# Adding two of six row sets by accumulating transfers, and reordering the end of a mixture-of-experts layer

## The chip, the cores and the metric

The kernel runs on one core of a Trainium2 chip. The metric is the time of one execution on the device in microseconds. A core has TensorE (PE) for products, VectorE (DVE) and ScalarE (ACT) for elementwise work, GpSimd (POOL) and SyncE (SP). Sixteen DMA engines serve the queues: SP's and ACT's are filled by hardware, POOL's by its own software.

## What is computed

Two layers of a transformer trunk on 512 positions of width 1024, in float32. Each layer has a token mixer of four attention branches, and then a mixture of experts. What matters here is the second half:

```python
h = rmsnorm(x, norm_ffn_g[l]) * (1.0 + sc2) + sh2
h2 = h.reshape(b * s, d)
y = swiglu(h2, w_shared_gu[l], w_shared_down[l]) + moe_routed(
    h2, router_w[l], router_bias[l], w_exp_gu[l], w_exp_down[l])
x = x + g2 * y.reshape(b, s, d)
...
return rmsnorm(x, final_norm_g)
```

Every token goes to 6 of 64 experts. `moe_routed` sums the six gated expert rows of each token. The next normalisation needs the mean of the squares of x per token.

## The kernel before, in words

x lies transposed on chip as `xT` (128 channels x 8 parts x 512 tokens). After the mixer and the shared expert, `pe_experts`, `act_experts`, `dve_experts`, `pool_experts` and `sp_experts` run the experts, one queue for each engine, joined by semaphores.

There are 65 blocks of up to 128 token rows, one for each expert and one, at position OV = 61 (line 49), for the rows of an expert that has more than 128; experts from 61 on come one block later. For a block, SP loads 3 MB of weights into one of four buffers `ew` (gate/up part 2 MB, L1528; down part 1 MB, L1531), and POOL gathers the rows of the block (L1640, L1651 for the overflow block). PE turns the rows (L2170), multiplies them by the gate/up weights in three products for each float32 product, of high and low parts (L2194), turns the activation (`turn_acted`, L2177) and multiplies by the down weights (L2213 and L2219, one half of the width each). ACT copies the result to `y` (`y_half`, L1395 and L1396). POOL scatters the rows to DRAM (`y_d`, L1674). Each row goes to the place (token, rank): rank r of a token is its expert in order of the expert's number. So the rows of rank 0 belong to experts up to 58, those of rank r to experts up to 58 + r. Before a gather or a scatter POOL waits on its semaphores and then reads the expert's row count, to choose a transfer of 64 or 128 rows (`by_count`).

The steps overlap: in step e PE turns the rows of block e+1, turns the activation of block e-1, does gate/up of e, and then down of e-1.

The end of the layer (`*_combine`) sums the ranks. SP loads each rank (512 rows of 4 KB, 2 MB) from `y_d` into a part of `ew` that is no longer used (`load_rank`, L1380 for ranks 0 to 3, L1383 for the halves of 4 and 5), each when the rows of that rank have landed (`wait_rows_landed`, L1376). All go through SP's queue in the order 0 to 5. DVE adds ranks 1 to 4 in two halves each to the sum in `up_of[1]` (`add_rank`, L1386) and rank 5 for each of the four blocks of 128 tokens (`last_rank`, L1453). For a token block t, PE turns the sum (`turn`, L1504), ACT scales it by the gate (`scaled`, L1425), DVE adds it to `xT` (`add_back`, L1458), ACT squares xT (`squares`, L1433, L1445), and PE multiplies the squares by a matrix of ones (`sums`, L1512). DVE picks the diagonal (`mean`, L1463) and POOL takes the root (L1416). The last token block is added by DVE straight from PSUM (L1488). Then the next layer begins, or, behind layer 1, the final scaling and the output.

Of the kernel before, what the change touches and what calls it, by code (L numbers as in the profile page):

```python
# [19 lines left out]
ALU = mybir.AluOpType  # L20
# [7 lines left out]
P = 128  # L28
# [20 lines left out]
OV = NE - 3  # L49
# [149 lines left out]
def hybrid_trunk(nc, xT_d, wmix_d, wexp_d, vec_d, gvec_d, cb_d, ada0_d, rw_d, vb_d, t5_d, const_d, rcst_d, onehot_d,  # L199
# [3 lines left out]
    with ctx:  # L203
# [1150 lines left out]
        with nc.Fori(0, L) as l:  # L1354
# [12 lines left out]
            ranks = [[up_of[i][:, 0:2], up_of[i][:, 2:4]] for i in (1, 2, 3, 0)] + [[down_of[1], down_of[2]], [down_of[3], down_of[0]]]  # L1367
            rank_sems = [rank_in[0:1], rank_in[0:1], rank_in[1:2], rank_in[2:3], [rank_in[3], rank_in[3]], [rank_in[4], over_in]]
# [8 lines left out]

            def load_rank(sp, r, sems_of):
                if r < 4:
                    sp.dma_start(up_of[(1, 2, 3, 0)[r]], y_rows[:, :, r, :]).then_inc(sems_of[0], 16)  # L1380
# [25 lines left out]
            def sp_combine(sp):  # L1406
                sp.wait_ge(ysum, 2)
# [10 lines left out]
            def act_combine(act):  # L1418
# [10 lines left out]
                def squares(t):  # L1429
                    act.wait_ge(yadd, t + 1)  # L1430
                    if t >= 2:
                        act.wait_ge(ysq_sum, t - 1)
                    nc.scalar.activation(sqc[t % 2][:], xT[:, :, t * P:(t + 1) * P], ACT.Square).then_inc(ysq_ready, 1)  # L1433

                scaled(0)
                scaled(1)
                squares(0)
                scaled(2)
                squares(1)
                squares(TC - 2)  # L1440
                for b in range(2):
                    act.wait_ge(yadd, TC + b)
                    if b == 0:
                        act.wait_ge(ysq_sum, TC - 2)
                    nc.scalar.activation(sqc[(TC - 1) % 2][:, 4 * b:4 * b + 4, :],  # L1445
                                         xT[:, 4 * b:4 * b + 4, (TC - 1) * P:], ACT.Square).then_inc(ysq_ready, 1)

            def dve_combine_rows(dve):
# [1260 lines left out]
```

## Time and profile before

| | us |
|---|---|
| median of 3 runs | 2917.96 |
| lowest, highest | 2916.21, 2921.76 |
| the profiled execution | 2920.52 |
| its span, first to last instruction | 2918.9 |
| mean granted TensorE clock | 0.978 of 2.4 GHz |

Times in the rows are microseconds from the start of the span; layer 0 ends near 1467 and layer 1 near 2907. A row of a timeline gives start, duration, engine, line, operation, and output <- input; xN says that N like instructions are merged, and the brackets say how long the engine had been idle and for what. The page shows the busy share of the engines over the whole execution. The work around the change is in the last 70 us of each layer, so the timelines of these stretches are read.

### The profile page before, as it was taken

How to read it: one execution, taken by the hardware profiler on the slowest of the kernel's cores; microseconds unless marked ns; L12 is line 12 of the kernel's file. 1: busy time of each engine (PE TensorE's matmuls, PEld its weight loads, DVE VectorE, ACT ScalarE, POOL GpSimd, SP SyncE). 2: the span in 40 equal slices, each digit the busy share in tenths (PEclk: the TensorE clock that was granted, in tenths of full speed). 3: DMA queues.
4: the chain of work that ended last, by engine and by line, in shares of the span. 5: the costliest groups of instructions: out<-in, count | busy, mean ns of one | idle time of the engine just before them, and what ended most of it. 6: DMA issues, size and time to landing. Idle time of an engine off the chain costs nothing. (4 is left out here: it accounts for less than half of the span.)

```text
span 2918.9 us, 42875 instructions
## 1 busy us (share of the span) xinstructions
PE 2766.5 (95%) x13980; PEld 2209.7 (76%) x13980; DVE 2079.3 (71%) x2849; ACT 1769.0 (61%) x2768; POOL 565.3 (19%) x567
## 2 busy tenths in 40 slices
PE   5999999999999999999789999999999999999995
PEld 4678777777778888888567777777777788888874
DVE  5544457565689999999855444566548999999987
ACT  2442434433569999999634334344335899999983
POOL 1000000100145533223110000000002555322221
PEclk9999999999999999999889999999999999999997
DMA  7224333234489999999722343423436999999986
GB/s 248 88 80 152 122 123 116 88 121 143 159 336 372 380 379 377 376 380 372 289 79 94 106 137 107 137 89 113 137 106 259 361 371 365 378 378 375 374 325 234
DMA packets 125102, 673.19 MB, mean 231 GB/s; under 512 B 27756, under 2 KB 29164, under 8 KB 90988
## 3 DMA queue, kind: packets, MB, share of 16 engines
q1 hardware_dynamic: 91328, 606.70, 56.1%
q0 software_dynamic: 31680, 58.36, 6.4%
q10 hardware_dynamic: 1932, 6.16, 0.9%
q8 instruction: 78, 1.28, 0.2%
q14 instruction: 84, 0.69, 0.1%
HBM read 657.39 MB, written 55.28 MB: 244 GB/s over the span
## 5 line engine op out<-in xcount | busy, mean ns | idle before, releaser
L1991 DVE TENSOR_TENSOR ew_lo<-ew,e_hi 128x2048 fp32r<-128x2048 f32 x258 | 590.5, 2289 | 53.9 <-ACT e_hi L1790 53.4
L759 PE MATMUL bank<-h_hi,w_hi 128*128 128x512 f32 x1216 | 493.2, 406 | 20.1 <-issue 5.5
L1790 ACT ACTIVATE e_hi<-ew 128x2048 fp32r<-128x2048 f32 x260 | 496.7, 1911 | 6.3 <-PE bank L2194 6.3
L759 PE MATMUL bank<-h_hi,w_lo 128*128 128x512 f32 x1216 | 487.4, 401 | 0.0
L759 PE MATMUL bank<-h_lo,w_hi 128*128 128x512 f32 x1216 | 484.4, 398 | 0.0
L694 DVE TENSOR_TENSOR w_lo<-raw,w_hi 128x1024 fp32r<-128x1024 f32 (+2 forms) x198 | 236.3, 1196 | 295.6 <-ACT w_hi L684 295.1
L2194 PE MATMUL bank<-e_hi,x_hi 128*128 128x512 f32 x1040 | 419.1, 403 | 0.1
L2194 PE MATMUL bank<-ew_lo,x_hi 128*128 128x512 f32 x1040 | 408.3, 393 | 0.0
L2194 PE MATMUL bank<-e_hi,x_lo 128*128 128x512 f32 x1040 | 406.0, 390 | 0.0
L759 PEld LDWEIGHTS bank<-h_hi,w_hi 128*128 128x128 f32 x1216 | 232.2, 191 | 93.5 <-issue 32.8
L684 ACT ACTIVATE w_hi<-raw 128x1024 fp32r<-128x1024 f32 (+2 forms) x198 | 202.9, 1028 | 148.8 <-PE bank L759 112.2
L759 PEld LDWEIGHTS bank<-h_hi,w_lo 128*128 128x128 f32 x1216 | 232.0, 191 | 64.9 <-issue 14.9
L759 PEld LDWEIGHTS bank<-h_lo,w_hi 128*128 128x128 f32 x1216 | 232.7, 191 | 54.8 <-issue 7.8
L1640 POOL DMA_INDIRECT xg<-h_d,idx x128 | 223.2, 1744 | 205.7 <-issue 193.4
L1090 ACT ACTIVATE pr<-sn,negmax 128x256 f32<-128x256 f32 (+3 forms) x256 | 137.0, 536 | 189.2 <-DVE negmax L1073 189.0
L1674 POOL DMA_INDIRECT y_d<-y,idx x130 | 130.4, 1003 | 564.5 <-issue 482.3
L2194 PEld LDWEIGHTS bank<-e_hi,x_lo 128*128 128x128 f32 x1040 | 195.7, 188 | 44.2
L2194 PEld LDWEIGHTS bank<-e_hi,x_hi 128*128 128x128 f32 x1040 | 195.9, 188 | 39.1 <-issue 0.5
L2194 PEld LDWEIGHTS bank<-ew_lo,x_hi 128*128 128x128 f32 x1040 | 196.2, 189 | 37.2
L2003 DVE TENSOR_TENSOR ew_lo<-ew,d_hi 128x1024 fp32r<-128x1024 f32 x128 | 157.1, 1227 | 28.8 <-ACT d_hi L1812 27.8
L1129 ACT ACTIVATE pt<-bank 128x128 f32<-128x128 f32 (+2 forms) x112 | 45.5, 406 | 203.7 <-PE bank L1155 183.2
L1984 DVE TENSOR_TENSOR x_lo<-bank,x_hi 128x512 fp32r<-128x512 f32 x260 | 166.4, 681 | 2.9 <-ACT x_hi L1782 2.8
(356 smaller groups left out, 4978.7 us busy)
## 6 DMA issues: line engine op xcount, KB each, us to landing
ew<-in_wexp SPq DMA_DIRECT2D x130, 2048.0 KB
raw<-in_wmix SPq DMA_DIRECT2D x297, 512.0 KB, 3.5
ew<-in_wexp SPq DMA_DIRECT2D x130, 1024.0 KB
ew<-y_d SPq DMA_DIRECT2D x8, 2048.0 KB, 11.7
ew<-y_d SPq DMA_DIRECT2D x8, 1024.0 KB, 7.3
ada0a<-in_ada SPq DMA_DIRECT2D x2, 2048.0 KB, 13.3
ada0b<-in_ada SPq DMA_DIRECT2D x2, 2048.0 KB, 22.1
h_d<-htok ACTq DMA_DIRECT2D x8, 512.0 KB, 2.7
```

The source lines that it names most:

```text
L684: ins = nc.scalar.activation(dst, src, ACT.Copy)
L694: ins = nc.vector.tensor_tensor(lo, src, hi.bitcast(F32), ALU.subtract)
L759: ins = nc.tensor.matmul(out, lhs, rhs, start=start, stop=stop)
L1090: nc.scalar.activation(prob(br, u)[:, 0:mp.nk], sn[u % 2][:, 0:mp.nk], ACT.Exp, bias=negmax[:, u:u + 1], scale=-1.0, accum_out=psum_of[:, ...
L1129: nc.scalar.activation(pt[0][:, 0:nk], TB[0][:, 0:nk], ACT.Copy).then_inc(pt_copied[0], 1)
L1640: nc.gpsimd.indirect_dma_start(out=xg[s][0:n, :], out_offset=None, in_=h2_d, in_offset=bass.IndirectOffsetOnAxis(ap=idx[j % 8][0:n, 0:1].b ...
L1674: nc.gpsimd.indirect_dma_start(out=y_d, out_offset=bass.IndirectOffsetOnAxis(ap=idx[j % 8][0:n, 1:2].bitcast(U32), axis=0), in_=y[j % 2][0 ...
L1790: nc.scalar.activation(e_hi[h][:], up_part(ew, j, h), ACT.Copy).then_inc(whi_done, 1)
L1984: nc.vector.tensor_tensor(x_lo[j % 2][:, 4 * b:4 * b + 4, :], TB[b][:].rearrange("p (k t) -> p k t", k=4), x_hi[j % 2][:, 4 * b:4 * b + 4, ...
L1991: nc.vector.tensor_tensor(up_part(ew_lo, j, h), up_part(ew, j, h), e_hi[h][:].bitcast(F32), ALU.subtract).then_inc(wlo_done, 1)
L2003: nc.vector.tensor_tensor(down_part(ew_lo, j)[:, :, 0:S], down_part(ew, j)[:, :, 0:S], hi[:, 0:2, :].bitcast(F32), ALU.subtract).then_inc( ...
L2194: ins = nc.tensor.matmul(G[s % 2][:], a, w, start=(h, k, i) == (0, 0, 0), stop=(h, k, i) == (1, 3, 2))
```

## The change

1. OV goes from 61 to 59: the overflow block stands two places earlier. SP's hand-written last steps start four blocks earlier so as to include it.
2. SP loads only ranks 0, 3, 4 and 5. Rank 0 needs the rows up to block 59 and the gate/up product of block 61. Rank 3 goes to `ew[2]`.
3. POOL adds ranks 1 and 2 to `up_of[1]` by accumulating transfers (`add_rows`), each behind the landing of the transfer before it. The two are issued after the scatters of blocks 61 and 62.
4. DVE no longer adds ranks 1 and 2. It waits for both transfers, adds ranks 3 and 4, then rank 5 for all four token blocks, and then does the adding back.
5. ACT's squares are gone. PE multiplies a block of xT by itself, and the diagonal of that product is the sum of squares.
6. In the last step PE does the first half of block 63's down product, the turning of block 64's activation, and then the second half. DVE's `down_low` is split in the same way, and ACT's `turned` for block 64 comes ahead of `y_half` for block 63.
7. 60 products whose result is not used (WARM) stand between the last down product and the first `turn`.
8. POOL reads the row count ahead of its waits (`count_of`).

```diff
-OV = NE - 3
+OV = NE - 5
+WARM = 60
...
-            ranks = [[up_of[i][:, 0:2], up_of[i][:, 2:4]] for i in (1, 2, 3, 0)] + [[down_of[1], down_of[2]], [down_of[3], down_of[0]]]
-            rank_sems = [rank_in[0:1], rank_in[0:1], rank_in[1:2], rank_in[2:3], [rank_in[3], rank_in[3]], [rank_in[4], over_in]]
+            ranks = [[up_of[i][:, 0:2], up_of[i][:, 2:4]] for i in (1, 1, 1, 2)] + [[down_of[1], down_of[2]], [down_of[3], down_of[0]]]
+            rank_sems = [rank_in[0:1], None, None, rank_in[2:3], [rank_in[3], rank_in[3]], [rank_in[4], over_in]]
...
+            def add_rows(pool, r, again=0):
+
+                pool.wait_ge(rank_in[0], 16 + 16 * again)
+                if r == 2 or again:
+                    pool.wait_ge(rank_in[1], 16 * (r - 1) + 32 * again)
+                pool.dma_start(up_of[1], y_rows[:, :, r, :], accum_op=ALU.add).then_inc(rank_in[1], 16)
...
-                link(dve, add_rank(1, 1))
-                dve.wait_ge(rank_in[1], 16)
-                link(dve, add_rank(2, 0))
-                link(dve, add_rank(2, 1))
-                dve.sem_inc(ysum, 1)
+                dve.wait_ge(rank_in[1], 32)
                 dve.wait_ge(rank_in[2], 16)
                 link(dve, add_rank(3, 0))
                 link(dve, add_rank(3, 1))
                 dve.wait_ge(rank_in[3], 32)
                 link(dve, add_rank(4, 0))
-                last_rank(0)
-                last_rank(1)
                 link(dve, add_rank(4, 1))
-                add_back(0)
-                last_rank(2)
-                add_back(1)
-                last_rank(3)
-                add_back(2)
+                for t in range(TC):
+                    last_rank(t)
+                for t in range(TC - 1):
+                    add_back(t)
...
                 def sums(t):
+                    own = (OB if t == TC - 1 else MB)[:, t * P:(t + 1) * P]
                     for b in range(2):
-                        pe.wait_ge(ysq_ready, t + 1 + (b if t == TC - 1 else 0))
+                        pe.wait_ge(yadd, t + 1 + (b if t == TC - 1 else 0))
                         for k in range(4 * b, 4 * b + 4):
-                            ins = nc.tensor.matmul((OB if t == TC - 1 else MB)[:, t * P:(t + 1) * P], ones[:], sqc[t % 2][:, k, :], start=k == 0,
-                                                   stop=k == KD - 1)
+                            x = xT[:, k, t * P:(t + 1) * P]
+                            ins = nc.tensor.matmul(own, x, x, start=k == 0, stop=k == KD - 1)
                     ins.then_inc(ysq_sum, 1)
 
+                for i in range(WARM):
+                    nc.tensor.matmul(TB[0][:], a_hi[0][:, 0, :], e_hi[0][:, 0, :], start=True, stop=True)
...
-                wait_rows_landed(sp, NE - 3)
-                sp.wait_ge(dn_ready, NE - 2)
-                load_rank(sp, 0, rank_sems[0])
...
+                for r in (0, 3, 4, 5):
+                    wait_rows_landed(sp, OV + r)
+                    if r < 4:
+                        sp.wait_ge(gu_used, 2 * (NE - 2 + r))
+                    else:
+                        sp.wait_ge(dn_ready, NE + 2 * r - 9)
+                    load_rank(sp, r, rank_sems[r])
...
                 for j in range(8):
                     step(NE // 8 - 1, j)
+                    if j >= 6:
+                        wait_rows_landed(pool, OV + j - 5)
+                        add_rows(pool, j - 5)
                 scatter(NE // 8 - 1, 7)
                 scatter(NE // 8 - 1, 8)
...
+                turned(NE // 8 - 1, 8)
                 y_half(act, NE // 8 - 1, 7)
-                turned(NE // 8 - 1, 8)
                 y_half(act, NE // 8 - 1, 8)
...
                     gate_up(e, j % 4)
-                    if not (first and j == 0):
+                    if last:
+                        down(e - 1, (j - 1) % 4, (0,))
+                        turn_acted(NE, 0)
+                        down(e - 1, (j - 1) % 4, (1,))
+                    elif not (first and j == 0):
                         down(e - 1, (j - 1) % 4)
```

## Rows read from the trace of the kernel before

**Rows 1.** The page: busy time of PE and its share of the span.

```profile
PE 2766.5 (95%) x13980; PEld 2209.7 (76%) x13980; DVE 2079.3 (71%) x2849; ACT 1769.0 (61%) x2768; POOL 565.3 (19%) x567
```

**Rows 2.** Timeline of PE at layer 1's end (columns as told above).

```profile
2861.43 0.39 PE L2213 MATMUL bank<-d_hi,a_hi 128*128 128x512 f32 x1
...
2866.72 0.50 PE L2213 MATMUL bank<-e_hi,a_hi 128*128 128x512 f32 x1 [2.14 <-DVE a_lo L2011]
2867.05 0.39 PE L2213 MATMUL bank<-ew_lo,a_hi 128*128 128x512 f32 x1
...
2869.34 0.39 PE L2219 MATMUL bank<-e_hi,a_lo 128*128 128x512 f32 x1
2887.87 3.65 PE L1504 MATMUL bank<-cst,ew 128*128 128x128 f32 x16 [18.14 <-DVE ew L1453]
...
2900.04 5.52 PE L1512 MATMUL bank<-sqc,ones 128*128 128x128 f32 x48
```

**Rows 3.** Timeline of DVE at layer 1's end.

```profile
2870.23 6.94 DVE L1386 TENSOR_TENSOR ew<-ew,ew 128x2048 f32<-128x2048 f32 x3 [1.37 <-issue]
...
2883.47 2.29 DVE L1386 TENSOR_TENSOR ew<-ew 128x2048 f32<-128x2048 f32 x1 [1.51 <-DMA ew<-y_d]
2886.50 2.36 DVE L1453 TENSOR_TENSOR ew<-ew,ew 128x1024 f32<-128x1024 f32 x2 [0.75 <-DMA ew<-y_d]
...
2892.42 1.22 DVE L1453 TENSOR_TENSOR ew<-ew,ew 128x1024 f32<-128x1024 f32 x1
...
2905.71 0.29 DVE L1463 CUSTOM_DVE_ANT_0 pick<-bank,cst 128x128 f32<-128x128 f32 x1 [0.93 <-PE bank L1512]
```

**Rows 4.** Timelines of PE and DVE at layer 0's end.

```profile
1430.46 0.50 PE L2213 MATMUL bank<-e_hi,a_hi 128*128 128x512 f32 x1 [2.14 <-DVE a_lo L2011]
...
1450.02 2.36 DVE L1453 TENSOR_TENSOR ew<-ew,ew 128x1024 f32<-128x1024 f32 x2 [0.70 <-DMA ew<-y_d]
...
1466.86 0.29 DVE L1463 CUSTOM_DVE_ANT_0 pick<-bank,cst 128x128 f32<-128x128 f32 x1 [0.93 <-PE bank L1512]
```

**Rows 5.** Timeline of SP's queue at layer 1's end: weights, then ranks.

```profile
2837.11 0.33 SPq L1531 DMA_DIRECT2D ew<-in_wexp  x1
...
2850.57 15.12 SPq L1380 DMA_DIRECT2D ew<-y_d  x4
2875.40 3.71 SPq L1383 DMA_DIRECT2D ew<-y_d  x4
```

**Rows 6.** Windows: stretch, length, busy us (instructions) by engine, clock, DMA share, GB/s.

```profile
2846.00:2851.00 5.00, 5.00 (x29) 4.23 (x28) 4.80 (x6) 4.62 (x9) 0.99 (x1) 1.00 0.02 2
...
2858.00:2863.00 5.00, 5.00 (x23) 4.11 (x22) 2.96 (x5) 2.79 (x5) 0.90 (x1) 1.00 1.02 406
...
2872.00:2874.00 2.00, 0.00 (x0) 0.00 (x0) 1.97 (x2) 0.00 (x0) 0.98 (x1) 0.54 0.93 371
...
2900.00:2902.00 2.00, 2.00 (x20) 2.00 (x19) 1.96 (x8) 0.23 (x1) 0.00 (x0) 1.00 0.00 0
```

**Rows 7.** Timeline of POOL: scatters of blocks 59, 61, 62, 63 and 64.

```profile
2830.24 0.91 POOL L1674 DMA_INDIRECT y_d<-y,idx  x1 [11.08 <-issue]
...
2848.28 0.99 POOL L1674 DMA_INDIRECT y_d<-y,idx  x1 [7.75 <-ACT y L1396]
2858.34 0.90 POOL L1674 DMA_INDIRECT y_d<-y,idx  x1 [9.06 <-issue]
2867.32 2.32 POOL L1674 DMA_INDIRECT y_d<-y,idx  x1 [8.08 <-issue]
2873.02 2.60 POOL L1674 DMA_INDIRECT y_d<-y,idx  x1 [3.39 <-issue]
```

**Rows 8.** Groups by line, POOL: a direct transfer from chip memory to chip memory.

```profile
L2331 POOL DMA_DIRECT2D kA<-kA x2 | 1.4, 686 | 14.4 <-DVE kA L2435 14.4
```

**Rows 9.** ACT at layer 1's end: a timeline row, then groups by line.

```profile
2870.26 0.59 ACT L1396 ACTIVATE y<-bank 128x512 f32<-128x512 f32 x1
...
L1425 ACT ACTIVATE sc<-bank,mod 128x128 f32<-128x128 f32 x24 | 6.4, 403 | 18.8 <-PE bank L1504 18.8
```

**Rows 10.** Timeline of PE in layer 1: turning the overflow block's rows.

```profile
2816.39 1.09 PE L2170 MATMUL bank<-cst,xg 128*128 128x128 f32 x8 [3.58 <-DMA xg<-h_d,idx]
```

More of the change, by code:

```diff
@@ L1427, in scaled @@
                         ins.then_inc(yscaled, 1)
[L1429 to L1446, printed above, removed]
+                for t in range(TC - 1):
+                    scaled(t)
             def dve_combine_rows(dve):
@@ L1475, in dve_combine_rows @@
                 link(dve, add_rank(4, 0))
-                last_rank(0)
-                last_rank(1)
                 link(dve, add_rank(4, 1))
-                add_back(0)
-                last_rank(2)
-                add_back(1)
-                last_rank(3)
-                add_back(2)
+                for t in range(TC):
+                    last_rank(t)
+                for t in range(TC - 1):
+                    add_back(t)
                 for b in range(2):
@@ L1551, in sp_experts @@
                 load_up(4, 0)
-                with sp.Fori(1, NE // 4 - 1) as it:
+                with sp.Fori(1, NE // 4 - 2) as it:
                     for j in range(4):
@@ L1562, in weights_of @@
                     return over if e == OV else expert_of(e)
-                for j in range(4):
-                    e = NE - 4 + j
+                for e in range(NE - 8, NE):
                     sp.wait_ge(gu_used, 2 * e - 4)
@@ L1600, in sp_experts @@
                         sp.wait_ge(o_wfree, i)
-                        for i_in, n in zip(rank_in, (32, 16, 16, 32, 16)):
+                        for i_in, n in zip(rank_in, (16, 32, 16, 32, 16)):
                             sp.wait_ge(i_in, n)
@@ L1609, in sp_experts @@
                     sp.wait_ge(o_turn, nb)
-                    sp.wait_ge(ysum, 1)
-                    for r in range(TOPK):
+                    for r in (0, 3, 4, 5):
                         load_rank(sp, r, rank_sems[r])
@@ L1637, in gather, with rows @@
                     pool.sem_inc(settled, 1)
-                    def rows(n):
+                    def rows(count):
                         nc.gpsimd.indirect_dma_start(
-                            out=xg[s][0:n, :], out_offset=None, in_=h2_d,
-                            in_offset=bass.IndirectOffsetOnAxis(ap=idx[j % 8][0:n, 0:1].bitcast(U32), axis=0),
+                            out=xg[s][0:count, :], out_offset=None, in_=h2_d,
+                            in_offset=bass.IndirectOffsetOnAxis(ap=idx[j % 8][0:count, 0:1].bitcast(U32), axis=0),
                             bounds_check=S - 1, oob_is_err=False).then_inc(xg_in[s], 16)
-                    by_count(e, rows)
+                    by_count(n, rows)
                 def gather_over():
@@ L1668, in scatter @@
                     e, s = 8 * it + j, j % 4
+                    n = count_of(e)
                     pool.wait_ge(yA, e + 1)
@@ L2091, in dve_experts @@
                                                 ALU.mult).then_inc(o_yD, 1)
-                    for i_in, n in zip(rank_in, (64, 32, 32, 64, 32)):
+                    for i_in, n in zip(rank_in, (32, 64, 32, 64, 32)):
                         dve.wait_ge(i_in, n)
                     dve.wait_ge(over_in, 48)
-                    add_rank(1, 0)
                 dve_combine_rows(dve)
@@ L2196, in gate_up, with down @@
                         ins.then_inc(gu_used, 1)
-                def down(e, s):
+                def down(e, s, halves=(0, 1)):
                     pe.wait_ge(alo_ready, e + 1)
@@ L2209, in down @@
                     high, high2 = (e_hi[0], e_hi[0][:, 2:4, 0:DSPLIT - S]) if end else (d_hi, d_hi2[:])
-                    for f in range(2):
+                    for f in range(2 if 0 in halves else 0):
                         for i, (a, w) in enumerate(((a_hi, high[:, f, :]), (a_hi, lo[:, f, 0:S]),
@@ L2214, in down @@
                                              stop=(f, i) == (1, 2))
+                    if 1 not in halves:
+                        return
                     pe.wait_ge(dlo_ready, 2 * e + 2)
```

63 lines of the change are left out of this document (27 added, 36 removed).

## The prediction

> **What bounds the kernel now.** I read the page first: PE is busy 95% of the span [rows 1], so little but its few idle stretches can be won; the largest inside a layer is the layer's end. The change touches only that end, in both layers, and a few instructions of the loop over experts before it. So I read layer 1's end engine by engine and took layer 0's as a second case.
>
> PE finishes the last block at 2869.7 and stands 18.14 us, until the first turn (transposes) at 2887.87 [rows 2]. The releaser is VectorE's last addition, L1453, which runs from 2886.50 after a short wait for a DMA [rows 3]. I call that moment T: 2886.5 in layer 1, 1450.0 in layer 0 [rows 3, 4], 19.8 and 19.6 us after the last block's down product begins (2866.72 and 1430.46 [rows 2, 4]). VectorE is busy for most of that time: additions of 2.3 us from 2870.23 on, with waits of 1.37, 1.51 and 0.75 us; the last two are for rows from DRAM [rows 3]. So VectorE and the transfers bound the end together; taking away additions alone would expose the transfers.
>
> The transfers: SP issues ranks 0 to 3 from 2850.57 to 2865.69, and the halves of ranks 4 and 5 from 2875.40 to 2879.11 [rows 5]. The DMA share is 0.02 in 2846 to 2851; with the rank loads under way it is 1.02 at 406 GB/s [rows 6]. A rank set of 512 rows of 4 KB, 2.1 MB, is thus 5.1 to 5.2 us of full engines. Ranks 4 and 5 wait for the scatters of the last two blocks (2867.32 and 2873.02 on POOL [rows 7]).
>
> **The change, part by part.** (a) The block for overflow moves from 61 to 59, so that rows of rank 0 are complete after block 59. Its scatter is at 2830.24 [rows 7]; SP is then free after its last weight load at 2837.11 [rows 5]. Rank 0 (5.1 us) is issued near 2838, behind 1 MB of weights, and lands near 2847.5, in the stretch whose share is now 0.02 [rows 6]. Of the six rank sets one leaves the busy stretch: worth 5.1 us of transfer.
>
> (b) Ranks 1 and 2 become accumulating transfers from POOL, one behind the other. POOL issues the first after block 61's scatter (2848.28 + 0.99 [rows 7]). Its issue: 0.69 us for a direct transfer of 224 pieces [rows 8]; here are 512, I take 1.0 to 1.2. Data starts near 2850.5. How long one add takes, a, is in no row. Lower bound: a plain read, 5.1 us. Upper bound: the engines read the held sum as well as the row, twice the bytes, 10.2 us. I take 7.0, nearer the plain read, since half of the reading is from the core's own memory and each row comes from DRAM once, as today; both ends are kept. (Below the plain read nothing is possible: the same bytes move.)
> The sum for T: first add 2850.5 to 2850.5+a, 1.0 to land, 1.1 to issue the second, so this begins at 2852.6+a. Rank 3 (5.1 us) shares the engines with it from about 2862.6: its rows need block 62's scatter and the last gate/up product, which ends at 2861.4 [rows 2]. Together they end at 2852.6+a+a+5.1. Then 0.8 to land (block 63's and 64's scatters, in POOL's queue behind the second add, land with it), 0.3+0.9 to issue and start rank 4, 5.1 for its data, 0.6 to land. VectorE, by then through with rank 3, needs 2 x 2.29 = 4.6 us for rank 4. T = 2870.0 + 2a. With a = 7.0 it is 2884.0, 2.5 us earlier in layer 1 and 2.3 in layer 0. With a = 5.1, the second add cannot start before block 62's scatter (2858.34 + 0.90 [rows 7]), and T is 2882.
>
> (c) VectorE loses four additions (9.2 us) ahead of T. Cover: it now waits for transfers, so these are already in T. Its last rank additions are done for all four row blocks first; T counts from the first of them, and four of 1.22 us [rows 3] end at T+4.7.
>
> (d) The last block: PE does half of block 63's down product before turning block 64, and ACT turns before it copies block 63. The 2.14 us gap [rows 2] shrinks to about 0.7, so the last product ends at about 2868.4. POOL reads the count before its waits: the scatter came 2.2 us after the copy that released it (2870.26+0.59 to 2873.02 [rows 7, 9]), put down to issue; I take 0.8 of it to remain. The last scatter is issued near 2870.3, 2.7 us earlier. At a = 7.0 all this hides behind the second add: zero; it counts only below a = 6. What is queued behind POOL's new waits are these scatters; the wait for the first add ends near 2858.5 and the scatter wants 2866, so it costs nothing until a exceeds some 15 us.
>
> (e) The 60 idle products. Ten starts of warm 512-column products lie 2.29 us apart (2867.05 to 2869.34 [rows 2]): 0.229 us each, 13.7 in all, 2868.4 to 2882.1. They end before turn 0 is possible (T+1.2), cost nothing there, and would delay it if T fell under 2881. What they buy is the clock. Before, it is granted 1.00 in 2858 to 2863, and 0.54 in 2872 to 2874, with PE idle since 2869.7: it fell from 2.4 to 1.2 GHz at the start of that stretch. It is back at 1.00 in 2900 to 2902 [rows 6]. After, the idle stretch is 2882.1 to T+1.2 = 2885.2, 3.1 us, about as long as the clock outlived the last product before (2869.7 to some 2872): even odds.
>
> (f) The end from T to the last mean: before 19.2 us in layer 1 (to 2905.71 [rows 3]) and 16.8 in layer 0 [rows 4]; I put the difference down to when the clock came back. After, ACT's passes of squares go. What is left: turn 0 and ACT's first scaling at T+2.5; 24 scalings in 6.4 us [rows 9] to T+8.9; the third add-back to T+10.2; then PE's sums. At the warm clock a sum of 16 instructions takes 1.84 (48 in 5.52 [rows 2]): sums 0 from T+6.0, turn 3, sums 1, 2, 3 back to back, last mean at T+14.5. At the cold clock (16 instructions of turns 0 and 1 took 3.65 [rows 2]) it is about T+16.5. Taking x itself as weights and as moving side costs what the ones did: same columns, same number of instructions. Gain: 2.3 and 4.7 us warm, 0.5 and 2.5 cold; I take 5 for both layers together.
>
> (g) Steady loop: the count read is moved only in POOL, which waits there; PE is bound by itself. One stall is exposed: 3.58 us at 2816.39, for the overflow block's rows [rows 10], absent in layer 0. It moves two blocks earlier and I take it as unchanged; it could vanish or come in both layers, -5 to +5 us with the cold products after it.
>
> **Sum.** (2.5 + 2.3) + 5 = 9.8 us. Against the profiled execution (2920.5, span 2918.9) that is 2910.7; the median of the runs is 2.5 lower, so 2908.2; I say 2908.
>
> **Rivals.**
> B, slower: each accumulating transfer reads twice, a = 10.2. For it: the engines already run at 400 GB/s whenever they run [rows 6]. Then T = 2890.4, 3.9 to 4.1 us late in each layer, the idle products end 9 us before turn 0, the clock is cold, and only 3 us come back at the end: +5 us, about 2923. It decides from a = 9.0: there T is 2888.0, 1.5 and 1.7 us late, which is all that the shorter end gives back, and each microsecond more of a costs 4 us of the whole. At a = 12 it is 2930.
> The Trainium skill (Collectives: The Full Stack, "The bandwidth ceiling: the fold count and why AG ≠ RS ≠ AR") says that an addition in a DMA needs two source reads on the same ring and halves the rate, 32.35 against 62.28 GB/s. By that rule a is 9.9 us here (an estimate by its ratio of 1.93) and the sum would be about 2922. No row of this trace shows an accumulating transfer.
> C, faster than forecast: a near 5.1 to 6. T = 2882, PE warm: 2 x 4.4 + 7 = 15.8 us, 2902. For it: the first add has idle engines to itself.
> D, no effect: with a from 8 to 9 the earlier transfer only pays for the adds, and PE is cold at turn 0: -4 to 0 us, about 2916. Against it: it is a narrow band of a.
>
> **Chances.** Forecast (a of 6 to 8) 0.34, C 0.20, D 0.20, B 0.26. C and most of the forecast are faster by over 0.2% (5.8 us, about what a measurement of this kernel can tell from no change); D is within it, with 0.02 of the forecast and 0.08 of B (a up to 10.4). Faster 0.52, same 0.30, slower 0.18. The range reaches from C with the stall of (g) gone in part, 2899, to B at a near 10.5, 2925.
>
> **What would show it.** Right: rank 0 issued near 2838, the first add's landing 7 to 8 us after its start, the second begun before 2861, the clock at 1.00 in the turns, no `sqc` rows, the last mean 14.5 to 16.5 us after the first last-rank addition. Wrong: rank 4 issued later than 2877, a scatter of block 63 that lands long after its issue, VectorE idle from 2866 to beyond 2880, or a second stall on the overflow block.

## The result and the profile after

The changed kernel takes 2931.6 us (2930.5 to 2933.9, 4 runs) beside 2917.1 for the kernel before in the same sessions (2915.4 to 2921.8, 4 runs); the ratio is 1.004, with a 95% interval of [1.0027, 1.0053]; the quotient of the two medians, 1.005, lies inside it. The changed kernel is slower by 0.4%, where 2908 was forecast, and it lies above the stated range (2899 to 2925). The profiled execution took 2930.45, with a span of 2928.8 and a mean granted clock of 0.982; 9.9 us more than the one shown of before.

VectorE at the end of layer 1, in the timeline of the changed kernel (against [rows 3]):

```profile
2868.45 1.22 DVE L1995 TENSOR_TENSOR ew_lo<-ew,e_hi 128x1024 fp32r<-128x1024 f32 x1
2887.24 4.62 DVE L1394 TENSOR_TENSOR ew<-ew,ew 128x2048 f32<-128x2048 f32 x2 [17.58 <-DMA ew<-y_d]
2895.80 2.29 DVE L1394 TENSOR_TENSOR ew<-ew 128x2048 f32<-128x2048 f32 x1 [3.94 <-DMA ew<-y_d]
...
2900.45 4.63 DVE L1444 TENSOR_TENSOR ew<-ew,ew 128x1024 f32<-128x1024 f32 x4
...
2915.24 0.29 DVE L1454 CUSTOM_DVE_ANT_0 pick<-bank,cst 128x128 f32<-128x128 f32 x1 [0.93 <-PE bank L1498]
```

Before, VectorE waited 1.37, 1.51 and 0.75 us there and added for the rest of the time; now it stands 17.58 us, until the second accumulating transfer has landed (rank 3 was there at 2881.1), and 3.94 for rank 4. T is 2900.45, 13.95 us later than before. Layer 0 shows the same: waits of 15.96 and 3.94 us, T at 1461.98 against 1450.02 [rows 4].

POOL in the same stretch (against [rows 7]), and SP's rank loads (against [rows 5]):

```profile
2851.91 0.91 POOL L1656 DMA_INDIRECT y_d<-y,idx  x1 [8.45 <-ACT y L1404]
2854.17 1.44 POOL L1384 DMA_DIRECT2D ew<-y_d  x1 [1.35 <-DMA ew<-y_d]
2861.30 1.12 POOL L1656 DMA_INDIRECT y_d<-y,idx  x1 [5.69 <-issue]
2868.52 1.34 POOL L1384 DMA_DIRECT2D ew<-y_d  x1 [6.09 <-DMA ew<-y_d]
2870.21 0.98 POOL L1656 DMA_INDIRECT y_d<-y,idx  x1 [0.35 <-issue]
2873.74 0.94 POOL L1656 DMA_INDIRECT y_d<-y,idx  x1 [2.54 <-ACT y L1404]
...
2843.60 25.17 SPq L1388 DMA_DIRECT2D ew<-y_d  x2
2887.74 2.16 SPq L1391 DMA_DIRECT2D ew<-y_d  x4
```

L1384 are the two adds. The first lands 13.4 us after its issue; POOL stands 6.09 us for it before it can issue the second, which lands 18.7 us after its own, near 2887.2. Rank 4's halves follow at 2887.74; before they were issued at 2875.40 [rows 5]. They wait for the rows of block 63: its scatter (2870.21) stands behind the second add in POOL's queue, and the trace has it landed at 2887.60, 17.4 us after its issue. In the same way block 62's scatter (2861.30) landed at 2868.28, just behind the first add, and rank 3's load, which needs those rows, was issued at 2868.40.

Why the adds take so long is in the windows of the changed kernel (columns as in [rows 6]):

```profile
2846.00:2851.00 5.00, 5.00 (x29) 4.23 (x28) 4.61 (x4) 4.31 (x6) 0.00 (x0) 1.00 0.92 369
2856.00:2861.00 5.00, 5.00 (x24) 3.85 (x23) 4.65 (x3) 4.31 (x8) 0.00 (x0) 1.00 0.99 177
2861.00:2866.00 5.00, 5.00 (x23) 4.11 (x22) 3.41 (x5) 2.81 (x4) 1.12 (x1) 1.00 1.07 213
2876.00:2881.00 5.00, 5.00 (x23) 4.13 (x22) 0.00 (x0) 0.00 (x0) 0.00 (x0) 1.00 1.05 247
2891.00:2896.00 5.00, 0.00 (x0) 0.00 (x0) 1.06 (x2) 0.00 (x0) 0.00 (x0) 0.50 1.02 410
```

With an add under way the engines are as full as ever (0.99) but move 177 to 213 GB/s; with plain loads alone they move 410 (last row; 406 before [rows 6]).

PE (against [rows 2]):

```profile
2868.59 0.51 PE L2199 MATMUL bank<-e_hi,a_hi 128*128 128x512 f32 x1 [0.55 <-DVE a_lo L2000]
...
2871.45 13.80 PE L1502 MATMUL bank<-e_hi,a_hi 128*128 128x512 f32 x60
2901.82 5.25 PE L1488 MATMUL bank<-cst,ew 128*128 128x128 f32 x24 [16.57 <-DVE ew L1444]
```

The gap ahead of block 64's down product is 0.55 us (2.14 before). L1502 are the 60 idle products. Behind them PE stands another 16.57 us.

To see where the 9.9 us went I divided the execution by marks that every timeline has: the last y copy on ACT, the last mean on VectorE, and in layer 1 the first and the 31st gather on POOL. Times in us, worked out as differences of such rows:

| kernel | layer 0: copy to mean | mean to first gather | 30 gathers | 31st gather to copy | layer 1: copy to mean |
|---|---|---|---|---|---|
| before | 31.4 | 770.0 | 272.3 | 361.1 | 35.4 |
| changed | 41.1 | 768.2 | 267.7 | 359.9 | 43.1 |

The layer's ends cost 9.7 + 7.7 = 17.4 us. The middle gave back 1.8 + 4.6 + 1.2 = 7.6. These are single profiles; the last column but one holds the wait for the overflow block's rows, 3.58 us before [rows 10] and 2.81 after.

### The profile page after: what moved, and what is told of

Read it like the earlier page. It is cut to its first block and busy times, and to the rows that moved or that the text cites. A ratio compares the mean times of both kernels' runs of the same rounds, so it can differ in the third digit from the quotient of the medians.

```text
span 2928.8 us, 43085 instructions
## 1 busy us (share of the span) xinstructions
PE 2787.3 (95%) x14100; PEld 2229.0 (76%) x14100; DVE 2062.4 (70%) x2841; ACT 1760.0 (60%) x2758; POOL 499.0 (17%) x571
## 5 line engine op out<-in xcount | busy, mean ns | idle before, releaser
L1617 POOL DMA_INDIRECT xg<-h_d,idx x128 | 171.9, 1343 | 136.5 <-issue 106.8
## 6 DMA issues: line engine op xcount, KB each, us to landing
ew<-y_d SPq DMA_DIRECT2D x4, 2048.0 KB, 11.3
```

The costliest lines, as they stand in the source:

```text
L1617: nc.gpsimd.indirect_dma_start(out=xg[s][0:count, :], out_offset=None, in_=h2_d, in_offset=bass.IndirectOffsetOnAxis(ap=idx[j % 8][0:count ...
```

## The experiments

"Before" in a ratio is always the kernel before, on the same chip in the same session.

**The adds replaced by plain transfers.** Same transfers, queue, waits and order. Ranks 0 and 1 are missing from the sum, since nothing is added.

```diff
-                pool.dma_start(up_of[1], y_rows[:, :, r, :], accum_op=ALU.add).then_inc(rank_in[1], 16)
+                pool.dma_start(up_of[1], y_rows[:, :, r, :]).then_inc(rank_in[1], 16)
```

> The changed kernel, with the two accumulating transfers as plain ones: same queue, same waits, same bytes from DRAM. The held sum is overwritten, so ranks 0 and 1 are left out of the result. Theory 1 (an accumulating transfer keeps the engines busy for more than twice as long as a plain one, and everything behind it is late): each of the two takes 5 to 6 us of engines instead of about 12, ranks 4 and 5 are issued some 10 us earlier, and the whole is 20 to 26 us shorter than the changed kernel, 2905 to 2912. Theory 2 (the rate is not it; the scatters of the last blocks stand behind POOL's transfers in one queue, and each of POOL's transfers waits for a landing): these waits all remain, the gain is under 8 us, 2923 or more.

Measured: 2911.8 us, ratio 0.9977 [0.9967, 0.9986]. VectorE in layer 1:

```profile
2869.54 4.62 DVE L1394 TENSOR_TENSOR ew<-ew,ew 128x2048 f32<-128x2048 f32 x2 [8.31 <-DMA ew<-y_d]
```

The wait is 8.31 instead of 17.58 us, and T stands 17.6 and 18.8 us behind the last y copy, against 26.7 and 28.3 in the changed kernel. The one argument that makes the transfer an adding one costs 9 us in each layer, 0.6% of the whole.

**SP loads all ranks, VectorE adds them.** No accumulating transfer. Ranks 1 to 3 get buffers of their own, and SP's loads for the next layer wait for VectorE's first additions; the rest of the change stays.

```diff
-                for r in (0, 3, 4, 5):
+                for r in range(TOPK):
...
-                dve.wait_ge(rank_in[1], 32)
+                dve.wait_ge(rank_in[0], 16)
+                dve.wait_ge(rank_in[5], 16)
+                link(dve, add_rank(1, 0))
+                link(dve, add_rank(1, 1))
+                dve.wait_ge(rank_in[1], 16)
+                link(dve, add_rank(2, 0))
+                link(dve, add_rank(2, 1))
+                dve.sem_inc(ysum, 1)
```

> The changed kernel without accumulating transfers: ranks 1 and 2 are loaded by SP into buffers of their own as they land, and VectorE adds them again; all else of the change stays (block 59, the order of the last block, own products, 60 idle products). Theory 1: VectorE then adds from 2866.5 (in the time of the kernel before) without a wait for 18.4 us, T is at 2885, the end is 2 to 4 us shorter: 2908 to 2912. Theory 2 (something else in the change, such as the place of the overflow block or the new order, costs the time): it stays at 2923 or more.

Measured: 2911.4 us, ratio 0.9969 [0.9956, 0.9982]. VectorE's timeline in layer 1:

```profile
2859.68 9.27 DVE L1395 TENSOR_TENSOR ew<-ew,ew 128x2048 f32<-128x2048 f32 x4
2869.10 4.62 DVE L1395 TENSOR_TENSOR ew<-ew,ew 128x2048 f32<-128x2048 f32 x2 [0.16 <-DVE ew L1395]
2874.12 2.29 DVE L1395 TENSOR_TENSOR ew<-ew 128x2048 f32<-128x2048 f32 x1 [0.40 <-DMA ew<-y_d]
```

VectorE now adds right behind the last block with one wait of 0.40 us. The four additions that the change took from it (9.27 us) were cheaper than the two transfers that replaced them.

**The transfers by themselves.** A core that does nothing else; SP and POOL move 2.1 MB in 4 KB pieces.

> The disputed cost by itself. Nothing of the model is computed; rows of 4 KB are put in DRAM with the same strides, and then transfers of 2.1 MB follow one another, each behind the landing of the one before: plain from SP, plain from POOL, accumulating from POOL in pieces of 4 KB and of 8 KB, 0.5 MB accumulating in pieces of 1 KB, accumulating from the core's memory to the core's memory, accumulating beside a plain load of SP, and plain from POOL. Theory 1: plain ones from either queue take 5 to 6 us of engines, accumulating ones 10 to 12.5 at any piece size from 4 KB up. Theory 2 (POOL's queue is the slow part): the plain transfer from POOL takes 8 us or more too.

Issues of POOL in its timeline; each but the first waits for the transfer before it:

```profile
58.89 0.90 POOL L42 DMA_DIRECT2D other<-y_d  x1 [58.45 <-DMA held<-y_d]
67.30 1.30 POOL L45 DMA_DIRECT2D held<-y_d  x1 [7.51 <-DMA other<-y_d]
80.90 1.20 POOL L48 DMA_DIRECT2D held<-y_d  x1 [12.30 <-DMA held<-y_d]
94.32 1.29 POOL L52 DMA_DIRECT2D held<-y_d  x1 [12.22 <-DMA held<-y_d]
101.11 1.26 POOL L55 DMA_DIRECT2D held<-other  x1 [5.49 <-DMA held<-y_d]
115.39 1.27 POOL L58 DMA_DIRECT2D held<-y_d  x1 [13.02 <-DMA held<-other]
133.28 0.76 POOL L61 DMA_DIRECT2D third<-y_d  x1 [16.62 <-DMA held<-y_d]
```

From issue to landing: plain (L42) 8.1 us, adding 13.3 (L45), with 8 KB pieces 13.1 (L48), a quarter of the bytes in 1 KB pieces 6.5 (L52), adding from on-chip memory 14.0 (L55). So neither pieces of 8 KB instead of 4 nor the source makes it cheaper. Nor is it POOL's queue: a plain transfer takes 8.1 and 7.9 us from POOL (L42, L61) and 7.4 from SP. Beside a plain load of SP the add takes 17.6 us (L58), and that load 11.9 instead of 7.4: until 120 only the load's data moves, and from then on each has about half of the bytes until the load ends.

**Sums of squares by a block's own product, alone,** in the kernel before (its diff is that of `sums` above, and ACT's squares go).

> The kernel before with one part of the change alone: sums of squares by the product of a block of x with itself, without ScalarE's squares. If the prediction's step on the end is right, the stretch from the first last-rank addition to the last mean is 1 to 2.5 us shorter in each layer, so 2912 to 2915 where the kernel before has 2917. If TensorE's own work sets the end, nothing changes (2916 to 2918).

Measured: 2918.8 us, ratio 0.9997 [0.9988, 1.0007]: nothing in the time. From T to the last mean it takes 16.45 us in layer 0 and 17.91 in layer 1, against 16.8 and 19.2 [rows 3, 4]; each is a single profile.

**One add instead of two.** Rank 1 by an accumulating transfer, rank 2 by SP and VectorE.

```diff
-                    if j >= 6:
+                    if j == 6:
                         wait_rows_landed(pool, OV + j - 5)
                         add_rows(pool, j - 5)
```

> The changed kernel, but only rank 1 is added by an accumulating transfer; rank 2 is loaded by SP as its rows land and added by VectorE, as two additions of 2.3 us. Theory 1, the chain of two accumulating transfers is too slow (13 to 14 us each), and one would fit before the last y copy: its single transfer is issued when rank 1's rows land, near 2856, and lands near 2869 to 2872 beside the loads; VectorE's wait behind the y copy at 2869.5 then falls from 17.6 us to 0 to 4 us, T comes near 2882, some 18 us earlier than in the changed kernel, and the time is 2908 to 2916 us (ratio to before 0.996 to 0.999). Theory 2, an accumulating transfer harms even alone, since it slows the rank loads and the weights beside it: T stays past 2890 and the time is 2920 us or more. Theory 3, the loss was the order of the loads and not the adds: the wait stays near 16 us and the time within 3 us of the changed kernel's 2931.

Measured: 2920.2 us, ratio 0.999 [0.9981, 0.9999]: 0.5% (15 us) below the changed kernel's ratio and 0.2% (6 us) above that without any add. The ratio is at theory 1's edge (0.999), but the time and T are those of theory 2 (2920 or more, T past 2890: it came at 2891.7, not 2882). Neither theory had the reason that the trace shows. The add, issued at 2853.98, lands 18.9 us later, and a new wait appears in ACT's timeline:

```profile
2873.63 0.60 ACT L1404 ACTIVATE y<-bank 128x512 f32<-128x512 f32 x1 [5.28 <-DMA y_d<-y,idx]
```

Block 64's y copy needs the buffer of block 62, whose scatter POOL issued at 2860.48, behind the add. It lands only near 2873, with the add (6.13 us of such waiting in layer 0).

**Does an add hold the scatter behind it?**

> No layer at all: transfers by themselves, on a core that does nothing else. POOL scatters 128 rows of 4 KB to DRAM alone, then straight behind a plain load of 2.1 MB, then straight behind an accumulating one; SP writes 0.5 MB of rows alone and beside an accumulating one; two accumulating transfers to two buffers are issued without a wait between them. Theory 1, POOL's queue is worked off in order in each engine, so that a scatter behind an accumulating transfer lands only with or behind it, 13 us or more after its issue (3 to 4 us alone, about 8 behind the plain load), while SP's write beside one lands in 3 to 6 us, and two adds take 26 us together. Theory 2, the engines share their time between transfers of all queues: the scatter behind the accumulating transfer lands in about 5 us, as SP's write does.

POOL's timeline, transfers of 2.1 MB and a scatter behind each:

```profile
61.73 0.79 POOL L60 DMA_DIRECT2D other<-y_d  x1 [2.65 <-DMA z_d<-y,idx]
62.82 1.00 POOL L49 DMA_INDIRECT z_d<-y,idx  x1 [0.30 <-issue]
71.97 1.37 POOL L64 DMA_DIRECT2D held<-y_d  x1 [8.14 <-DMA z_d<-y,idx]
73.64 1.04 POOL L49 DMA_INDIRECT z_d<-y,idx  x1 [0.30 <-issue]
```

L49 is the scatter of 0.5 MB. From issue to landing it takes 3.4 to 3.6 us alone, 8.9 behind the plain load (L60) and 13.0 behind the add (L64). So theory 1: the scatter is held by what stands ahead of it in POOL's own queue. SP's write of 0.5 MB takes 2.6 us alone and 2.7 when it is issued with an add, but this does not test the two side by side: in the trace the write's data moves from 90.0 to 92.0 and the add's only from 92 on. What the other queue suffers is in two other traces: a plain load of SP beside an add lands after 11.9 us, ahead of the add (above), and in the changed kernel rank 3 lands 6 us ahead of the second add, while block 63's scatter, a quarter of its size and issued 1.8 us later, lands with the add. Two adds issued without a wait between them land 23.0 us after the first issue (104.02 + 13.2, 104.81 + 22.2): the second costs 9.8 us more. That is the price of the data alone.

**Idle products: 126 instead of 60** in the changed kernel, so that PE works until T.

> The changed kernel with 126 idle products at the end of layer 1 in place of 60 (and as many more in layer 0), so that TensorE has work until T. Theory 1, the long wait for the ranks let the clock fall (0.50 in 2891 to 2896), but what follows T is bound by ScalarE's 24 scalings of 6.3 us and by VectorE's means as much as by TensorE: the granted clock is 1.00 after T, the first three turns take 3.3 to 4.3 us as before, T is where it was (2898 to 2901) and the end from T to the last mean goes from 14.8 to 13.5 to 14.5; time 2928 to 2931 us. Theory 2, the cold clock costs what it cost in the kernel before (19.2 at a low clock against 16.8): 2 to 3 us a layer, time 2925 to 2927 us. Theory 3, the products run past T and the turns queue behind them: 2933 us or more.

Measured: 2933.8 us, ratio 1.0054 [1.0039, 1.0069]: no gain on 1.004. The products end 1.88 us ahead of the first turn, and T to the last mean takes 14.45 us in layer 1 (14.8 with 60). The granted clock was 1.00 in 2904 to 2906, just ahead of the turns, where it was 0.50 with 60 products; behind the first turns it fell, to 0.61 in 2908 to 2912. Theory 1 had the stretch right, but the time lies above its range.

**No idle products** in the best form (below).

> The form in which SP loads the ranks 0 to 3 as their rows land, VectorE adds them and the indices come early (2906.6 us), without the 60 idle products at the layer's end. Theory 1, they bring a warm clock for the turns and sums: without them the turns take 3.6 us per 16 and T to the last mean goes from 14.4 to 16.5 or more, so that the time is 3 to 5 us higher, 2909.5 to 2911.5. Theory 2, their clock is gone again before T (the granted clock was 0.50 at the first turn in either case) and comes back by the turns themselves: T to the last mean stays within 0.5 us, the time within 1.5 us of 2906.6.

Measured: 2906.9 us, ratio 0.9951 [0.9938, 0.9963], against 0.995 [0.9937, 0.9963] with them. T to the last mean: 14.4 and 15.1 us without, 14.8 and 14.5 with. They bring nothing that can be measured.

**Sums and 80 idle products** in the kernel before.

> The kernel before with two parts of the change alone: the squares' sums by a block's own product, and 80 idle products between the last down product and the turns. With the sums alone the time was 0.9997 of before's, and 16.45 us from T to the last mean in layer 0. Theory 1, the sums gain only where TensorE's clock is full: with the idle products T to the last mean falls to 14.4 to 14.8 us in both layers (16.8 and 19.2 before), and the time is 4 to 6 us below before's: ratio 0.998 to 0.9987. Theory 2, the short end of the changed kernel came from its other parts (the reordered last block, the earlier vector loads): 16 us or more stay, and the time is within 2 us of before's.

Measured: 2921.9 us, ratio 1.0008 [0.9997, 1.0019]; T to the last mean 19.0 and 18.8 us. Theory 1 falls. PE in layer 0:

```profile
1454.07 2.14 PE L1494 MATMUL bank<-cst,ew 128*128 128x128 f32 x16 [0.27 <-DVE ew L1443]
1459.71 1.97 PE L1494 MATMUL bank<-cst,ew 128*128 128x128 f32 x8 [3.50 <-DVE ew L1443]
1461.47 3.62 PE L1503 MATMUL bank<-xT 128*128 128x128 f32 x16
```

The first 16 turns run at full clock (2.14 us). PE then stands 3.50 us, the granted clock goes to 0.64 in 1458 to 1460 and 0.50 (1.2 GHz) in 1460 to 1464, and the 16 products of the first sum take 3.62 us instead of 1.95. Filling the time ahead of T did not help, because the kernel before has its own gap behind T.

**The overflow block at 59** in the kernel before, and nothing else.

> The kernel before with one part of the change alone: the overflow block runs as block 59 and not as block 61. Theory 1, the end of the layer is bound by what follows the last y copy (16.7 us to T), which the place of the overflow block does not touch: only the wait for its rows moves, by up to 3 us either way; time within 3 us of before's. Theory 2, the earlier last slot blocks let the ranks be filled and loaded earlier: 3 us or more below before's. Theory 3, the place costs: the wait, 0 in layer 0 and 3.6 in layer 1 before, becomes 2 and 3 to 5 us as in the changed kernel, and the time is 2 to 4 us above before's.

Measured: 2919.9 us, ratio 0.9997 [0.9986, 1.0008]; the wait for its rows is 3.4 us in layer 1 (3.6 before): it moved and kept its size.

**The early read of the row count** in the kernel before, and nothing else.

> The kernel before with one part of the change alone: POOL reads the row count ahead of its waits. Theory 1, the read (about 1 us) stood between the wait and the transfer, so that gathers came late for TensorE now and then (six waits of 0.2 to 0.6 us among the first 30 blocks of layer 1, 7.5 us of waits for rows in all, none in the changed kernel's same stretch), and the last scatter as well: 3 to 8 us below before's time, ratio 0.997 to 0.999. Theory 2, as predicted blind, TensorE is bound by itself in the loop and only POOL waits: within 2 us of before's, ratio 0.9995 to 1.0005.

Measured: 2922.4 us, ratio 1.0002 [0.9991, 1.0013]. The 30 gathers take 268.2 us in this profile, as in the changed kernel (267.7) and not as in before (272.3), so the middle of the layer did get 4.1 us shorter. The stretch behind them is 4.0 longer (365.1), half of it the wait for the overflow block's rows, 5.6 us here. Locally theory 1, in the time theory 2.

**The overflow block's indices one block earlier,** in three kernels.

```diff
-                    if e + 1 == OV:
+                    if e + 2 == OV:
```

In the changed kernel:

> The changed kernel with one thing altered: SP loads the overflow block's indices one block earlier. Theory 1, the wait for the overflow block's rows (7.2 us in all in the changed kernel) is SP's late index load alone and has nothing to do with the accumulating transfers: it falls to 1 to 2 us, the waits of VectorE for ranks stay at 16 to 18 us, and the time is 5 to 6 us below the changed kernel's: 2925 to 2927. Theory 2, the time gained in the loop is lost again at the layer's end, whose adds do not begin earlier: within 2 us of 2931.

Measured: 2935.2 us, ratio 1.0052 [1.0039, 1.0065]. PE's waits for rows fall from 7.2 to 2.1 us and the time does not follow: the ratio is not below the changed kernel's 1.004, and theory 1 falls. POOL does this:

```profile
2862.70 1.44 POOL L1384 DMA_DIRECT2D ew<-y_d  x1 [10.59 <-DMA ew<-y_d]
2864.44 0.98 POOL L1656 DMA_INDIRECT y_d<-y,idx  x1 [0.30 <-issue]
2877.71 1.34 POOL L1384 DMA_DIRECT2D ew<-y_d  x1 [12.29 <-DMA ew<-y_d]
```

Rank 0 landed 18.9 us after its issue (10.0 in the changed kernel), POOL stood 10.59 us for it, and the scatters stood behind POOL's wait. The layer's ends take 45.6 and 45.3 us (41.1 and 43.1 in the changed kernel). Full engines do not explain rank 0: the DMA share was 0.35, 0.10 and 0.11 in 2850 to 2865. The trace has a transfer's landing in sixteen parts: thirteen were there 8.1 us after the issue, the last three after 13.1, 13.9 and 18.9 us (in the changed kernel thirteen after 7.7, the last after 10.0). The three weight loads ahead of it have such a tail too, their last parts 17 to 24 us after the issue. Why a few parts came so late is open.

With ranks loaded by SP and added by VectorE:

> No accumulating transfer and no addition by POOL: SP loads each of the ranks 0 to 3 when its rows land, VectorE adds them, and SP loads the overflow block's indices one block earlier. Theory 1, the two effects are separate: the loads and additions as in the form without the early indices (T 16.0 us behind the last y copy in layer 0 and 16.0 in layer 1), and the wait of TensorE for the overflow block's rows (6.6 us in all there, 1.4 us once the indices came early) goes; the time is 4 to 6 us below that form's 2911.4: 2905 to 2908 us, ratio to before 0.994 to 0.996. Theory 2, the ranks' loads, started earlier, meet the weights and the stall comes back there: 2910 us or more.

Measured: 2906.6 us (2902.0 to 2907.3), ratio 0.995 [0.9937, 0.9963]. It is the fastest form found, 12.6 us under before's median of the same session (2919.2). Its interval overlaps that of the form without the early indices (0.9969 [0.9956, 0.9982]), so that step is not shown apart here. It is in the next pair.

**POOL adds rank 1 itself,** without and with the early indices.

```diff
+                    if j >= 6:
+                        pool.wait_ge(rank_in[0], 16)
+                        pool.wait_ge(rank_in[5], 16)
+                        nc.gpsimd.tensor_tensor(ranks[0][j - 6], ranks[0][j - 6], ranks[1][j - 6], ALU.add).then_inc(pchain, 1)
```

> All ranks are loaded by SP as their rows land, no accumulating transfer, and of the two early ranks one is added by POOL itself (two additions over 2048 columns) ahead of the last scatter, the other by VectorE; 55 idle products. Against the form in which VectorE adds both (2911.4, T at 2878.8 in layer 1): theory 1, VectorE's queue of additions from the last y copy to T sets T, so that two of its 2.3 us additions fewer bring T 4.6 us earlier a layer if the last rank's rows are there, bounded by the landing of ranks 4 and 5: 3 to 9 us in all, time 2903 to 2908. Theory 2, POOL's additions delay its own scatters or VectorE's operations beside them by as much (the page of the trace has no addition by POOL of this size; one over 2048 columns may take 4 to 10 us): time 2910 us or more. Theory 3, the last ranks' landing sets T, and it is where it was: 2909 to 2912.

> As the form with POOL's additions, and the load of the overflow block's indices is issued one block earlier by SP, so that its gather can be issued earlier. Theory 1, the stall of TensorE and VectorE on the overflow block's rows (3.6 us before, 1.8 to 5.1 us a layer in the forms since) is the late index load, queued on SP behind the weights: it falls to under 1 us a layer and the time is 2 to 6 us below the form without it. Theory 2, the gather is late for POOL's own order or the count: stall and time stay within 1 us. Theory 3, the stall goes and comes back as a wait for ranks at the layer's end, since their landing sets T: the loop ends earlier and T stays.

Measured: 2923.8 us, ratio 1.0011 [1.0003, 1.002], and with the early indices 2917.0, ratio 0.9991 [0.9982, 0.9999]: the indices bring 6.8 us, and PE's waits for rows go from 10.3 to 1.4 us in all. Against the same forms with VectorE's additions (and 60 idle products instead of 55) the ratios are 0.42 and 0.41% higher, 12 us: theory 2 of the first expectation. POOL, then VectorE, in layer 1 of the first of the two:

```profile
2864.24 4.68 POOL L1705 TENSOR_TENSOR ew<-ew,ew 128x2048 f32<-128x2048 f32 x1 [8.53 <-DMA ew<-y_d]
...
2864.86 5.15 DVE L2001 TENSOR_TENSOR ew_lo<-ew,d_hi 128x1024 fp32r<-128x1024 f32 x1 [0.39 <-ACT d_hi L1809]
2869.93 1.21 DVE L2005 TENSOR_TENSOR ew_lo<-ew,d_hi 128x1024 fp32r<-128x1024 f32 x1
```

A subtraction of 1.22 us, begun 0.6 us after POOL's addition, ends about a microsecond after it: it took 5.15. It feeds block 63's down product. The Trainium skill (SBUF — State Buffer, "Who interferes with whom") says that a VectorE instruction with two inputs from on-chip memory contends with a GpSimd instruction that reads it, and that such contention is an exclusive lock; the row agrees. The next such subtraction, beside POOL's second addition, takes 5.18 us, and PE stands 2.16 and 3.61 us in its last two down products (0.55 in the changed kernel). With the early indices, POOL's additions bring the last y copy 5.6 us later in layer 0 and lengthen the stretch from the 31st gather to it by 8.7 in layer 1, while T follows the copy 2.0 and 3.4 us sooner. So the loss lies ahead of the last y copy, where the stretched subtractions are; that they alone make up the 12 us was not tested.

## Why the prediction was wrong, point by point

**(a) Rank 0 early: half right.** The transfer did move into the idle stretch (share 0.92 where 0.02 was [rows 6]). But it was issued at 2843.60, not 2838, and landed after 10.0 us, beside the weights. What SP waited for was the landing of block 59's scatter, issued at 2833.00 and landed at 2843.44: 10.4 us, where the same scatter took 7.9 before (2830.24 to 2838.10). My sum had no term for it. The first add was issued 4.9 us later than in my sum (2854.17 against 2849.3). Only 1.35 us of this is POOL's wait for rank 0; 3.6 us is that block 61's scatter, from which the sum starts, came later (2851.91 against 2848.28). In layer 0 rank 0 landed at 1415.18 and the add was issued at 1415.92, right behind the scatter: no wait for rank 0 at all.

**(b) The length of an add: the step that failed.** I took a = 7.0, nearest to the plain read, "since half of the reading is from the core's own memory". The transfers by themselves speak against this reason: from on-chip memory an add is no faster (14.0 against 13.3), and the data of a queued one costs 9.8 us, about my upper bound of 10.2. The row that was nearest in distance (a plain read) was not nearest in mechanism; nothing in the trace spoke for 7. The Trainium skill's rule beside rival B (Collectives: The Full Stack, "The bandwidth ceiling: the fold count and why AG ≠ RS ≠ AR") gave 9.9 as an estimate, from the rates of two collectives; the 9.8 agrees.

But a at 9.8 gives only about 2921 by rival B's line (4 us of the whole for each microsecond of a). The sum was also short in its other parts. For layer 1, forecast against measured: first add issued +4.9 (see (a)); its landing 13.4 us after the issue instead of 9.2, +4.2; the wait until the second's issue, +0.9; the second together with rank 3, 18.7 instead of 14.0, +4.7; rank 4, 8.6 instead of 6.9, +1.7. Together 16.4, which is 2900.4 against 2884.0. The same five in layer 0 are 2.9, 4.4, 0.9, 4.3 and 1.7, together 14.2. So the two adds are 8.9 and 8.7 us of it, the largest part, and the step that failed is their term a. Counted as in my sum (1.1 to issue, 1.0 to land), the first add is a = 11.3, and rival B's own line gives 2927 for that and 2930 at a = 12. Its mechanism was right, its likeliest price too low, and my range ended below its upper end. The signs that I had named for being wrong all came: rank 4 issued at 2887.74 (later than 2877), block 63's scatter landed 17.4 us after its issue, VectorE idle from 2869.7 to 2887.2, and a second stall on the overflow block (1.8 us, in layer 0).

**(c) Four additions off VectorE: right, and worth nothing.** They were cover. With them back, and only plain loads, T is 16.6 us behind the last y copy in layer 1 (16.2 before); with the adds it is 28.3.

**(d) The last block: right.** The gap went from 2.14 to 0.55 us (0.7 forecast), and the last scatter followed its copy by 1.0 us (2872.14 + 0.59 to 2873.74; 2.2 before). Both hid behind the adds, as said.

**POOL's waits: "costs nothing until a exceeds some 15 us": wrong in kind.** POOL's own waiting cost little in the changed kernel, but for block 62's scatter, behind the first add, I looked only at when it is issued. What is issued behind an add also lands behind it. So rank 3's load came at 2868.40 and not near 2862.6; what this cost by itself no run shows, since the add kept the engines full meanwhile (share 0.99 and 1.07). In the form with one add ACT had to wait for such a landing, 5 to 6 us a layer.

**(e) The idle products: length right (13.8 us), worth nil.** The clock was at 0.50 in 2891 to 2906, since T was so late. But neither products nearly up to T, with the clock at 1.00 for the first turns, nor none at all (in the best form) made a difference clear of noise. With 60 products the clock came back during the turns and sums: 0.79 in 2906 to 2908, 1.00 in 2908 to 2912.

**(f) From T to the last mean: right number, wrong reason.** 14.8 and 14.4 us came out for 14.5. I credited this to the vanished squares and the clock. But the kernel before has an addition of rank 4 (2.29 us) just behind T, and the changed kernel has it ahead of T; without it, before's 16.8 is 14.5. So by these two profiles nothing was gained in layer 0 and 2.1 us in layer 1. How much of that is the profile's chance is open: two kernels that differ from before only elsewhere (the block at 59, the early count) take 17.9 and 19.3 us in layer 0, and 19.3 in layer 1. My sum stayed whole, since it had both additions of rank 4 in T, but most of the gain of part (f) was only T's moved mark. The sums alone brought nothing in the time.

**(g) The loop: unchanged as forecast only in the sum.** The wait for the overflow block's rows is now in both layers (1.8 and 2.8 us, where it was 0 and 3.6), and PE's waits for rows are 7.2 us in all against 7.5. I said of the count read "moved only in POOL": it shortened 30 blocks by 4.6 us. In the kernel before PE waited six times 0.2 to 0.6 us for rows there, which I had not read, since I looked at the layer's last 70 us only.

**The rivals.** D asked for a between 8 and 9 and falls with it; C falls with a below 6. The range should have gone to a of 12, named in rival B, since the fixed costs of a transfer that no row shows have no upper bound in the rows; even that gives 2930, just short of the measured 2931.6.

Open: why the wait for the overflow block's rows differs between profiles of like kernels (0 to 5.7 us in layer 1), where the count read's gain goes in detail, and which part of the change carries the gain of the best form: the sums, the block at 59 and the early count brought nothing alone, and the reordered last block and the early rank loads were not run alone.

## What to carry to other kernels

Moving an addition into a transfer does not remove it: on engines that are the bound it is the dearer place, here 9.8 us of full DMA engines for 4.6 us of VectorE. When an operation has no row, take the bound whose mechanism is reasoned (bytes read and written), and measure it by itself first. A part worth keeping can hide in a change that loses: here the rest of the change, with the ranks loaded as their rows land, the additions left on VectorE and the indices early, gives 0.995.

## What the hardware showed unexpectedly

- With an accumulating transfer under way the DMA share is 0.99 to 1.07 at 177 to 213 GB/s, where plain ones reach 406 to 410. By itself it is 195 to 207 GB/s with pieces of 4 KB, 198 with 8 KB and 183 from on-chip memory, at a share of 1.01 to 1.06.
- A scatter of 0.5 MB lands 13.0 us after its issue behind an add in POOL's queue (3.5 alone), while a plain load of 2.1 MB in SP's queue beside an add lands after 11.9 (7.4 alone), ahead of the add.
- An add issued with a plain load of SP moves no data of its own at first: issued at 115.39, its data starts near 120.
- An addition on POOL of 4.7 us stretched a VectorE instruction with two inputs from 1.22 to 5.15 us.
- The granted clock fell within a gap of 3.50 us, although TensorE had worked at full clock for 18.3 us of idle products and 2.14 us of turns just ahead of it; the 16 products behind the gap took 3.62 us instead of 1.95.
